# Gated DeltaNet and mLSTM layer: the inverse's levels on 64 columns, gate products woven between them, another order in head 0, two raw weight buffers

## What is computed

```
proj = h @ w_in                       # 1088 x 1024 @ 1024 x N
cv   = silu(causal_conv(qkv_b))       # 4 taps
q_b, k_b = l2norm(cv_q), l2norm(cv_k)
# per head and chunk of 64 tokens:
m_kk  = where(strict, kb @ k.T * decay, 0)
a_mat = m_kk + eye                    # unit lower triangular
sol   = triangular_solve(a_mat, [v*beta, kb*exp(gam)])
u = w_v - w_k @ S;  o = q_dec @ S + qk @ u
S = S * g_last + k_dec.T @ u          # scan over the chunks
hb = head_rms(hb) * g_norm_b * silu(z_b)
```

## Time and profile before

| | us |
|---|---|
| median of three runs | 2831.93 |
| profiled execution, its own time | 2830.69 |
| its span | 2829.0 |
| TensorE busy | 2615.4 (92%) |
| DVE busy | 1168.1 |
| ACT busy | 645.5 |
| POOL busy | 636.1 |

### The profile page before, as it was taken

How to read it: one execution, slowest core, us unless ns; L and a number is a source line. 1 busy time by engine, 2 the same in 40 slices (tenths; PEclk the granted TensorE clock), 3 DMA queues, 4 the chain that set the end, 5 groups by cost and what they waited for, 6 DMA issues and landing times.

```text
span 2829.0 us, 40488 instructions
## 1 busy us (share of the span) xinstructions
PE 2615.4 (92%) x16191; PEld 2542.3 (90%) x16191; DVE 1168.1 (41%) x1930; ACT 645.5 (23%) x1322; POOL 636.1 (22%) x321
## 2 busy tenths in 40 slices
PE   3779999999998799999589999999999999999997
PEld 2769999999997799998489999999999999999897
DVE  4565556556544143453421312654223123134534
ACT  4535454545444111111100000011001000010112
POOL 2332121221210111110122321442212212212421
PEclk7889999999999899999799999999999999999998
DMA  3131221122201316523611211211111111111211
GB/s 131 27 94 43 63 71 54 40 70 63 63 9 31 94 39 95 86 48 53 123 45 44 101 45 44 101 45 45 45 45 45 45 39 52 45 38 45 68 35 67
DMA packets 235322, 165.33 MB, mean 58 GB/s; under 512 B 23211, under 2 KB 222443, under 8 KB 235151
## 3 DMA queue, kind: packets, MB, share of 16 engines
q1 hardware_dynamic: 217414, 154.69, 19.7%
q10 hardware_dynamic: 17792, 8.95, 2.3%
HBM read 135.84 MB, written 27.76 MB: 58 GB/s over the span
## 4 chain that ended last, share of the span: by engine, by line
PE 46%; DVE 2%; issue 1%; DMA 1%; POOL 1%; ACT 0%; POOLq 0%; DVEq 0%; ACTq 0%
PE bank L227 41%; PE bank L239 4%; PE bank L2609 1%; DVE t_rlo L2745 0%; DMA t_w_raw<-in_w_in_dram 0%; PE bank L2646 0%; POOL t_w_lo L216 0%; DVE t_rhi L2742 0%; DVE hlo L2771 0%; DVE hhi L2768 0%; POOL t_rlo L2457 0%; DMA t_rraw<-HB 0%; PE bank L2521 0%; DVE hraw L2915 0%; DVE t_x L2837 0%
## 5 line engine op out<-in xcount | busy, mean ns | idle before, releaser
L216 POOL TENSOR_TENSOR t_w_lo<-t_w_raw,t_w_hi 128x1024 fp32r<-128x1024 f32 x112 | 270.0, 2411 | 953.1 <-DVE t_w_hi L211 953.1
L227 PE MATMUL bank<-t_rlo,t_w_hi 128*128 128x384 f32 (+1 forms) x1248 | 409.5, 328 | 4.6 <-issue 4.6
L227 PE MATMUL bank<-t_rhi,t_w_lo 128*128 128x384 f32 (+1 forms) x1248 | 409.4, 328 | 2.5 <-issue 2.5
L227 PE MATMUL bank<-t_rhi,t_w_hi 128*128 128x384 f32 (+1 forms) x1248 | 409.2, 328 | 0.0
L227 PE MATMUL bank<-hhi,t_w_lo 128*128 128x384 f32 (+1 forms) x1224 | 399.6, 327 | 2.5 <-POOL t_w_lo L216 2.5
L227 PE MATMUL bank<-hhi,t_w_hi 128*128 128x384 f32 (+1 forms) x1224 | 399.7, 327 | 0.0
L227 PE MATMUL bank<-hlo,t_w_hi 128*128 128x384 f32 (+1 forms) x1224 | 399.5, 326 | 0.0
L227 PE MATMUL bank<-hhi,b_w_lo 128*128 128x384 f32 (+1 forms) x768 | 272.1, 354 | 11.4 <-POOL b_w_lo L216 11.4
L227 PE MATMUL bank<-hhi,b_w_hi 128*128 128x384 f32 (+1 forms) x768 | 253.8, 330 | 0.0
L227 PE MATMUL bank<-hlo,b_w_hi 128*128 128x384 f32 (+1 forms) x768 | 253.5, 330 | 0.0
L227 PEld LDWEIGHTS bank<-t_rlo,t_w_hi 128*128 128x128 f32 x1248 | 236.1, 189 | 5.2 <-issue 5.1
(11 more groups left out here) (377 smaller groups left out, 4346.2 us busy)
## 6 DMA issues: line engine op xcount, KB each, us to landing
b_w_raw<-in_w_in_dram SPq DMA_DIRECT2D x32, 512.0 KB, 4.0
t_w_raw<-in_w_up_dram SPq DMA_DIRECT2D x32, 512.0 KB, 3.9
t_w_raw<-in_w_down_dram SPq DMA_DIRECT2D x32, 512.0 KB, 3.9
a_w_raw<-in_w_in_dram SPq DMA_DIRECT2D x24, 512.0 KB
t_w_raw<-in_w_in_dram SPq DMA_DIRECT2D x16, 512.0 KB, 3.7
b_gam<-ROWS_B SPq DMA_DIRECT2D x8, 576.0 KB, 5.0
b_kb<-ROWS_B SPq DMA_DIRECT2D x8, 576.0 KB, 3.6
b_eg<-ROWS_B SPq DMA_DIRECT2D x8, 576.0 KB, 3.5
```

Of the source, the lines that this page charges most:

```text
L216: pool.tensor_tensor(self.lo[j % 2][:, 0:kt, :], self.raw[j % self.rs][:, 0:kt, :], self.hi[j % 2][:, 0:kt, :], ALU.subtract).then_inc(sel ...
L227: ins = pe.matmul(out, a[:, k, :], b[:, k, :], start=(start and k == 0 and i == 0), stop=(stop and k == kt - 1 and i == 2))
```

## The change

1. **Levels on 64 columns.** At each level only half of the columns of the inverse change. "z" and "e" now multiply only these: the moving operand has 64 columns a chunk, the stationary one still 128 (`scores_of`, `inverse_of`). The masks are half as large, DM is packed to 64 columns a chunk, ACT's evictions (`evict_half`) and DVE's masking touch half. The unit columns of Z are written by POOL (`unit_columns`, four a head), and Z has two buffers, QN and WKT. The transposes into the last level use 64 columns for 5 of 8 chunks, and "e0" has 8 transposes instead of 9 (`turned_of`).
2. **Weaving.** Groups 1 and 2 of the output gate's product are no longer made ahead of the levels but step by step (3 matmuls a step, 16 steps, `spare`) between the phases: 3 steps after "vt", 2 after the first "z", 1 after each other phase, 2 after the last "e". The norms of the next head's K go one group each behind three phases. ACT applies the SiLU to these two groups before and behind the evictions of "wk". The cast of the next head's V slab moves from behind the first level to the end of the head, and POOL's subtraction with it, in front of the next head's `unit_lower`.
3. **Other moves.** DVE's exponents go in thirds over the levels, the further taps of K's convolution stand ahead of the keys; ACT has exponentials and decays both behind the transposes into the last level.
4. **Head 0.** Its V groups 0 and 1 stand ahead of the gate's norm, the output gate is at position 3 and K at position 4, and the output gate's slab is requested ahead of the gate's stores. ACT's `gate.columns`, `replicas` and SiLUs stand in another order to fit. Head 0 has no woven steps.
5. **mLSTM.** `raw_slots=2`.

```diff
+NORM_AT = (("e", LOW), ("d", LOW), ("z", LOW + 1))
...
+SPARE = {("vt", LOW): 3, ("z", LOW): 2, ("e", LEVELS - 1): 2}
...
-    SM = sb("b_sm", [P, LEVELS - LOW, P])
+    SM = sb("b_sm", [P, LEVELS - LOW, P // 2])
...
-    Z = QN
...
+    Z = (QN, WKT)
...
             slab(0, V_, 2, 0)
+            slab(0, Z_, 3, 0)
             gate.stores(sp)
             for i in (0, 2, 1):
                 row(0, i)
-            slab(0, K_, 3, 1)
...
-            slab(0, Z_, 4, 0)
+            slab(0, K_, 4, 1)
...
+            def unit_columns(h, l):
+                out = halves(Z[(l - LOW) % 2][:, 0:SEQ], l, 1, NC)
+                src = halves(ident[:], l, 1, 1).to_broadcast([P, NC, P >> (l + 1), 1 << l])
+                pool.tensor_tensor(out, src, src, ALU.mult).then_inc(unity.sem, 1)
...
                 if nxt:
                     WS.split_lo(pool, h + 1, 1)
+                read(pool, h, ("p2", 2))
+                wait(pool, qd, h, 1)
+                unit_columns(h, LOW)
+                if scan:
+                    SB.taken(pool, h - 1, ("u", NC))
+                    wait(pool, masked, h - 1, 1)
+                unit_columns(h, LOW + 1)
+                read(pool, h, ("e", LOW, 2))
+                unit_columns(h, LOW + 2)
+                read(pool, h, ("e", LOW + 1, 2))
+                unit_columns(h, LOW + 3)
+                if nxt:
                     WS.split_lo(pool, h + 1, 2)
 
             WS.split_lo(pool, 0, 3)
...
+            def scores_of(h, l):
                 for t in range(3):
                     if l == LOW:
                         wait(pe, diag, h, 2 * t + 2)
-                    of_chunks(h, ("z", l, t), AT, DM, [("e0", t) if l == LOW else ("d", l - 1, t)], n=parts(t))
+                    bank = claim(h, ("z", l, t), ("e0", t) if l == LOW else ("d", l - 1, t))
+                    for i in range(parts(t)):
+                        c = 3 * t + i
+                        ins = pe.matmul(bank[:, 64 * i:64 * i + 64], AT[:, c * L:c * L + L], DM[:, 64 * c:64 * c + 64],
+                                        start=True, stop=True)
+                    filled(ins, h, ("z", l, t))
...
+            def inverse_of(h, l):
+                wait(pe, unity, h, l - LOW + 1)
                 for t in range(3):
-                    of_chunks(h, ("e", l, t), Z, E, [("z", l, t)], n=parts(t))
-                if l < LEVELS - 1:
-                    for t in range(3):
-                        of_chunks(h, ("d", l, t), E, None, [("e", l, t)], transpose=True, n=parts(t))
+                    bank = claim(h, ("e", l, t), ("z", l, t))
+                    for i in range(parts(t)):
+                        a = (3 * t + i) * L
+                        ins = pe.matmul(narrow(bank[:, 64 * i:64 * i + 64], l, 1)[:, 0], Z[(l - LOW) % 2][:, a:a + L],
+                                        halves(E[:, a:a + L], l, 1, 1)[:, 0], start=True, stop=True)
+                    filled(ins, h, ("e", l, t))
...
+            def turned_of(h, name, l):
+                for t in range(3):
+                    slot = name + (t,)
+                    bank = claim(h, slot, *([("e", l - 1, t)] if l > LOW else []))
+                    for i in range(parts(t)):
+                        a = (3 * t + i) * L
+                        if l == LEVELS - 1 and i:
+                            ins = pe.transpose(bank[:, 64 * i:64 * i + 64], E[0:64, a:a + L], ident[0:64, 0:64])
+                        else:
+                            ins = pe.transpose(bank[:, L * i:L * i + L], E[:, a:a + L], ident[:])
+                    filled(ins, h, slot)
...
                 turned(h, "kt", KN)
                 wait(pe, kn, h, 2)
                 products(h, "p2", KN, QN)
-                if nxt:
-                    whole(h, Z_, 1, h, 4)
                 wait(pe, silus, h, 3)
                 turned(h, "vt", VS)
-                if nxt:
-                    whole(h, Z_, 2, h, 4)
+                fill(more, "vt", LOW)
+                levels(h, nxt, more)
+            def fill(more, n, l):
+                for _ in range(SPARE.get((n, l), 1)):
+                    next(more, None)
+            def spare(h, pos):
+                for g in (1, 2):
+                    a, w = GROUPS[g]
+                    out = SB.claim(pe, h - 1, ("spare", g))[:, 0:w]
+                    for k in range(KT):
+                        ins = WS.product(pe, pos, out, hhi[:, :, a:a + w], hlo[:, :, a:a + w], kt=k + 1, first=k,
+                                         stop=(k == KT - 1))
+                        if k == KT - 1:
+                            SB.filled(ins, ("spare", g))
+                        yield
+            def levels(h, nxt, more=iter(())):
                 for l in range(LOW, LEVELS):
-                    level(h, l)
-                    if nxt and l == LOW:
-                        norm(h, h + 1, K_)
+                    for n in ("z", "e", "d"):
+                        if n == "z":
+                            scores_of(h, l)
+                        elif n == "e":
+                            inverse_of(h, l)
+                        elif l < LEVELS - 1:
+                            turned_of(h, ("d", l), l + 1)
+                        else:
+                            break
+                        for slot in normed_at(nxt, n, l):
+                            norm(h, h + 1, K_, slot[2])
+                        fill(more, n, l)
+                for _ in more:
+                    pass
                 for t in range(3):
...
+                for g in range(2):
+                    whole(0, V_, g, 0, 2)
                 pe.wait_ge(s_mask, MASKS)
                 gate.taken(pe)
                 norm(-2, 0, K_)
                 for g in range(NG):
                     taken(pe, -1, ("dense", K_, g))
-                for g in range(NG):
-                    whole(0, V_, g, 0, 2)
+                whole(0, V_, 2, 0, 2)
                 for g in range(NG):
                     taken(pe, -2, ("n", K_, g))
                 gate.turned(pe)
+                for g in range(2):
+                    whole(0, Z_, g, 0, 3)
                 norm(0, 0, Q_)
-                whole(0, K_, 0, 0, 3)
                 wait(pe, kb, 0, 1)
                 products(0, "p1", KN, KB)
+                whole(0, Z_, 2, 0, 3)
+                whole(0, K_, 0, 0, 4)
+                replicated(0)
                 for g in range(1, NG):
-                    whole(0, K_, g, 0, 3)
-                replicated(0)
-                for g in range(NG):
-                    whole(0, Z_, g, 0, 4)
+                    whole(0, K_, g, 0, 4)
...
+            def z_spare(h, g):
+                a, w = GROUPS[g]
+                src = SB.read(act, h - 1, ("spare", g))
+                SB.release(act.activation(ZS[:, a:a + w], src[:, 0:w], ACT.Silu), ("spare", g))
...
+            def levels(h, nxt, scan):
                 for l in range(LOW, LEVELS):
                     for t in range(3):
-                        evict(h, ("e", l, t), E, parts(t))
+                        evict_half(h, ("e", l, t), E, l)
+                    if nxt and l == LOW + 1:
+                        log(h, K_, 2)
                     if l < LEVELS - 1:
                         for t in range(3):
-                            evict(h, ("d", l, t), DM, parts(t))
+                            evict_half(h, ("d", l, t), DM, l + 1)
                     if nxt and l == LOW:
-                        logs(h, K_)
-                    if nxt and l == LOW + 1:
+                        for g in range(2):
+                            log(h, K_, g)
+                    if nxt and l == LOW + 2:
                         exps(h, K_)
-                    if nxt and l == LOW + 2:
                         decays(h + 1)
+                if scan:
+                    z_spare(h, 1)
                 for t in range(3):
                     evict(h, ("wk", t), WKT, scale=-1.0)
+                if scan:
+                    z_spare(h, 2)
...
-                keys(h, scan)
-                scores(h)
                 if nxt:
                     for i in range(1, W):
                         conv(h + 1, K_, i)
+                keys(h, scan)
+                scores(h)
                 values(h)
-                rest(h, nxt)
-
-            def rest(h, nxt):
...
+            def rest(h, nxt, scan):
+                for l in range(LOW, LEVELS):
+                    level(h, l, scan)
+                    if nxt and l == LOW:
+                        taken(dve, h, ("vt", 2))
+                        scalars(h + 1)
+                    if nxt and l < LEVELS - 1:
+                        exponents(h + 1, l - LOW)
                 if nxt:
                     unit(h + 1, K_, KN)
                     scaled_k(h + 1)
                 masks(h)
+                if nxt and scan:
+                    SB.read(dve, h - 1, ("spare", 2))
+                    WS.split_hi(dve, h + 1, 2, None, after=())
+                elif nxt:
+                    split(h + 1, 2, h, K_)
...
```

(2 more changed lines are left out.)

158 lines of the change are left out of this document (89 added, 69 removed).

## The result

| | before | changed |
|---|---|---|
| median of six runs, us | 2832.06 (2828.44 to 2833.84) | 2820.52 (2818.24 to 2824.0) |
| profiled execution's span, us | 2829.0 | 2818.7 |

The account below looks back on a forecast made before the run. TensorE was taken as almost always busy in looped heads, with idle mainly in head 0 and the mLSTM. Head 0 -10, looped heads +3, last head +2, mLSTM -18 sum to -23: 2830.69 - 23 + 1.24 = 2809 us, range 2788 to 2828.

Parts of the forecast that it names:

- mLSTM, -18: mLSTM stage: a second raw buffer removes 12.7 us of waits for low halves and 5.1 of slow clock (-14 to -20).
- 64 columns save nothing: Level phases z and e: fp32 matmuls moving 64 columns take 0.11 to 0.12 us a record, as with 128.
- the first rival: Levels: 64 columns really are cheaper, 6.3 us a head, 50 in all, 2759 us; chance 0.12.
- 0.3 us saved by narrow transposes: Each head: five 64-column transposes into the last level and one transpose fewer at the start save 0.3 us.
- Woven work costs TensorE nothing: Levels: output-gate groups 1 and 2 are the same matmuls moved, free for TensorE, and cover 0.45 us of small waits.
- Waits in the looped heads: Looped heads: V's transposes wait 0.5 us for DVE's keys, the scan 0.7 for DVE's state; six heads net +3.
- Head 0, -10: Head 0: reordering cuts TensorE's idle from 26.0 to 12.6 us, less 2.5 of losses: -10 us (-4 to -16).
- (a): Head 0: V's groups 0 and 1 ahead of the norms cover 8.5 of 8.7 us waiting for ACT's logarithms; 0.2 left.
- (b): Head 0: position 3's slab, requested before the gate's stores, has its low half ready at 137.1; 4.5 us of wait left.
- (c): Head 0: K's slab, at position 4, has its low half ready at about 161; 8.7 us of wait left.
- the second rival: Levels: the clock falls, two levels at half speed cost 7.1 us a head, 57 in all, 2866 us; chance 0.09.
- The third rival: DeltaNet moves bring nothing: head 0 gains 0, looped heads lose 1.5 us each; -7 in all, 2825 us; chance 0.16.

Follow-up runs that it names:

- the first two runs: Kernel before with two raw mLSTM weight buffers: 2812.61 us, ratio 0.9918; changed kernel with one raw buffer there: 2842.54 us, ratio 1.0025.
- the padded kernel before: Kernel before, one raw buffer, with 24 unread matmuls added in the last head: 2816.57 against 2825.66 us, ratio 0.9974.

## Why the prediction was right or wrong, point by point

- **mLSTM, -18: right**, with the mechanism. It was 20.0 in the two traces, and 20.6 and 21.7 in the first two runs against their counterparts with the other number of buffers. It is not the same on every chip: in the padded kernel before the waits for low halves were 2.7, 3.2 and 2.0 us, and the mLSTM took 435.0 against 422.0 with two buffers, 13.
- **64 columns save nothing: right.** The window of weight loads was what it rested on, and the run with 128 columns gave 97.93 against 97.91. The 0.063 us of the narrow transposes did not carry over. In head 0 the narrow phases may even have cost some 3 us by the clock (one trace). The Trainium skill, "TensorE: Matmul & The Clock Gate", section "LDWEIGHTS (loading the stationary operand)", lets a load depend on the stationary columns alone; the trace agrees, with 0.112 us from record to record at either width. Its section "Back-to-back issue gap", the first rival's rule, has the gap halve with the columns, and says itself that the formula counts too little for small matmuls, whose loads are not in it. Half of 0.112 would have had the looped heads 7 us shorter (the prediction's 0.05 x 128 x 8 is 51, not 55).
- **0.3 us saved by narrow transposes: wrong in sign.** The step "up to 0.06 each between the same two spacings" took spacings from streams of one shape. The mixed eight took 1.46 against 0.79.
- **Woven work costs TensorE nothing: wrong.** Each of 12 places costs about 0.1 us of change-over (0.54 for a step against 0.44). It gives back 0.08 in each of eight phases (1.70 at 64 and at 128 columns, against 1.78 in the kernel before) and the 0.45 of small waits, and without it, in the changed order, a head at full clock is 2.2 us longer. I had counted only the 0.45.
- **Waits in the looped heads: partly right.** V's transposes waited 0.35 a head for the keys (0.5 forecast). The 0.49 for the logarithm was not in the sum: a bank of z follows the norm's in the ring and waits for ACT, and I had not followed the ring over the new norm places. The 0.7 for DVE's state did not come: unit-lower starts 6.1 us behind the levels (6.7 forecast), and the scan kept its length. Six heads: +6.7 instead of +3.
- **Head 0, -10: the steps to the first z were nearly right, the rest was not.** The first z came 10.9 us sooner, not 12.6: the waits of (a) and (b) were 0.2 and 4.6 as forecast, that of (c) 7.6 in two pieces, 1.3 of it for ACT, instead of 8.7; but 5.5 in three waits for DVE and ACT behind them stood in no term, 4.0 of it for the scores. The check by DVE's chain had the first e near 190; it came at 192.5. The failing step is "about 1 us of slow clock": the wait for the scores took the clock to half for z, e, norms and transposes, and again at "wk", so that the part from the first z to the next head's woven products took 33.5 us instead of 25.8. With the clock kept full it took 26.1, and head 0 was at -10.5. The total was -3.1 here and in one more trace, and -4.5 to -4.9 in four others of the same head 0. With it the second rival (slow clock in the levels) was right in this one head. Looped heads showed it only when the order on DVE was made worse, and one of them without the woven steps.
- **Last head, +2: too small,** +1.4 up to "wk" and +2.3 behind it. The second is a wait of 1.0 us for ACT's SiLU of the woven group, and slow clock in the scan behind it (0.92). It varies: in the other traces of changed kernels the last scan took 51.1 to 54.9, against 50.0 to 50.2 with the DeltaNet code of before.
- **Tail, 0: +2.4 here,** out of the stall at the loop's ends (4.15 and 4.15 against 3.7 and 3.4) and the clock behind it.
- **The third rival, nearest of all.** It had DeltaNet at +11 (0 + 9 + 2) and 2825 us; measured were +7.3 and 2820.5, where the forecast had -5 and 2809. It was given 0.16. Its +9 for the looped heads came near (+6.7); its reason for head 0, a DVE chain that ends where it did, did not hold, since z came 10.9 us sooner.
- **The prediction's own signs.** It called itself wrong if looped heads differ by over 1.5 us (1.1 measured), if the clock is under full in the levels (in head 0 it was, 0.80), or if head 0 gains under 4 (3.1 measured).

Sum by terms: -20.0 - 3.1 + 6.7 + 3.7 + 2.4 = -10.3. The median fell into the range because the range ran up to 2828: the three DeltaNet terms ended at or near their bad ends, and the mLSTM's at its good one.

## What to carry to other kernels

Price an instruction between others of another shape or type by a row where they alternate, not by a stream of its own kind: narrower work cost more here. An idle gap of 3.8 us on TensorE cost 7.3 in the looped heads, so an edit that lets TensorE arrive early at something another engine is late with can give much of its gain back (7.7 of 10.9 us in head 0). Try the smallest edit of a bundle alone: here one line held more than the whole gain.

## What the runs showed of the hardware that was not expected

- 24 unread matmuls far ahead of the tail shortened it by 9 to 12 us (1435 to 1437 in seven traces, 1445 to 1448 in eleven): idle of 0.9 to 1.4 us at the two ends of a loop instead of 3.4 to 4.4, and full clock behind them. The one ratio taken for it alone was 0.9974. Two kernels can differ by 0.3% in code that neither changed; compare stages before crediting an edit.
- Alternating transposes of 128 and of 64 columns (64 partitions) took 0.18 us each in the mean, equal ones 0.10; two narrow ones in a row were 0.11 apart.
- The fp32 matmul with 64 moving columns took as long as with 128: 0.112 us from record to record, 1.70 us a phase, in both.
- Behind 4.0 us of idle, z and e of 128 moving columns took 3.4 and 1.8 us (one trace). With 64 columns e took 3.4 in all nine traces that idled there for 3.1 to 4.9 us.
